# The down projection of two squared-ReLU MLPs as seven block products in place of eight, in a one-core Trainium2 kernel

## What is computed

```
D_MODEL = 1024; SEQ = 512; D_FF = 4 * D_MODEL
...
def mlp_sq_relu(h, w1, w2):
    return jnp.square(jax.nn.relu(h @ w1)) @ w2
...
        h = h + mlp_sq_relu(rms_norm_2(h, norm2[i]), mlp_w1[i], mlp_w2[i])
```

## Time and profile before

| | before |
|---|---|
| timed runs, median of 3 | 2932.26 us |
| lowest and highest | 2931.02 and 2935.89 us |
| the profiled execution: span | 2930.3 us |
| instructions | 51243 |
| PE busy (matmuls) | 2753.7 us, 94% |
| PEld busy (weight loads) | 2152.7 us, 73% |
| DVE busy | 1123.4 us, 38% |
| ACT busy | 916.9 us, 31% |
| POOL busy | 781.5 us, 27% |
| DMA | 397.00 MB, mean 135 GB/s |

### The profile page before, as it was taken

One profiled execution on the slowest core, in us unless ns is written; L12 is line 12 of the kernel. 1 busy time (PEld: TensorE's weight loads), 2 busy tenths in 40 slices (PEclk: granted clock), 3 DMA queues, 4 the chain that ended last, 5 costly groups with the idle time before them and its releaser, 6 DMA issues. The chain is left out here.

```text
span 2930.3 us, 51243 instructions
## 1 busy us (share of the span) xinstructions
PE 2753.7 (94%) x22943; PEld 2152.7 (73%) x22943; DVE 1123.4 (38%) x1554; ACT 916.9 (31%) x1458; POOL 781.5 (27%) x216
## 2 busy tenths in 40 slices
PE   7999989888989998888999999989999999999999
PEld 5877878778774333334899989987888888888887
DVE  5435765664552111114543475353211124431111
ACT  4133242343351000002355445543322232242222
POOL 2321332132120000001322332312444434434443
PEclk9999999999999999999999999999999999999999
DMA  7112201103165999996312221221332323322331
GB/s 276 53 33 63 65 4 63 62 3 106 48 244 223 424 426 427 427 427 257 128 58 73 72 86 54 78 72 58 101 101 88 99 87 101 99 88 89 100 101 58
DMA packets 171436, 397.00 MB, mean 135 GB/s; under 512 B 9519, under 2 KB 99604, under 8 KB 145876
## 3 DMA queue, kind: packets, MB, share of 16 engines
q1 hardware_dynamic: 170240, 390.34, 36.4%
q10 hardware_dynamic: 980, 3.40, 0.3%
HBM read 387.36 MB, written 4.19 MB: 134 GB/s over the span
## 5 line engine op out<-in xcount | busy, mean ns | idle before, releaser
L186 POOL TENSOR_TENSOR weight_ring_lo<-weight_ring,weight_hi 128x2048 fp32r<-128x2048 f32 (+1 forms) x144 | 656.9, 4562 | 1788.2 <-ACT weight_hi L175 1745.4
L175 ACT CAST weight_hi<-weight_ring 128x2048 fp32r<-128x2048 f32 (+1 forms) x144 | 271.4, 1886 | 550.1 <-PE late L244 309.9
L244 PE MATMUL late<-weight_hi,latT_hi 128*128 128x512 f32 x572 | 175.3, 429 | 0.0
L225 PE MATMUL late<-latT_lo,weight_hi 128*128 128x512 f32 x680 | 167.9, 389 | 0.0
L225 PE MATMUL late<-latT_hi,weight_ring_lo 128*128 128x512 f32 x680 | 167.9, 389 | 0.0
L225 PE MATMUL late<-latT_hi,weight_hi 128*128 128x512 f32 x680 | 167.9, 389 | 0.0
L244 PE MATMUL late<-weight_ring_lo,latT_hi 128*128 128x512 f32 x572 | 156.6, 396 | 0.0
L244 PE MATMUL late<-weight_hi,latT_lo 128*128 128x512 f32 x572 | 155.8, 394 | 0.0
L225 PEld LDWEIGHTS late<-latT_hi,weight_ring_lo 128*128 128x128 f32 x680 | 127.6, 188 | 26.5
L225 PEld LDWEIGHTS late<-latT_lo,weight_hi 128*128 128x128 f32 x680 | 127.6, 188 | 26.5
L225 PEld LDWEIGHTS late<-latT_hi,weight_hi 128*128 128x128 f32 x680 | 127.6, 188 | 26.5
(11 more groups left out here) (696 smaller groups left out, 5226.8 us busy)
## 6 DMA issues: line engine op xcount, KB each, us to landing
weight_ring<-in_mlp_w SPq DMA_DIRECT2D x64, 1024.0 KB, 5.3
weight_ring<-in_w_gate SPq DMA_DIRECT2D x41, 1024.0 KB, 15.2
weight_ring<-in_w_down SPq DMA_DIRECT2D x38, 1024.0 KB, 15.2
weight_ring<-in_w_up SPq DMA_DIRECT2D x36, 1024.0 KB, 12.7
weight_ring<-in_a_wqkv SPq DMA_DIRECT2D x36, 1024.0 KB, 5.0
weight_ring<-in_w_mod SPq DMA_DIRECT2D x24, 1024.0 KB, 5.7
weight_hi_spare<-in_w_up SPq DMA_DIRECT2D x16, 1024.0 KB, 12.5
weight_hi_spare<-in_w_down SPq DMA_DIRECT2D x16, 1024.0 KB, 15.1
```

Of the source, the lines that this page charges most:

```text
L175: self.nc.scalar.copy(self.view(self.hi[:, q % 2], p, True), self.view(self.slots[self.slot[p]], p, True)).then_inc(self.hi_ready, 1)
L186: self.nc.gpsimd.tensor_tensor(self.view(self.lo[:, s], p, True), self.view(self.slots[s], p, True), self.view(self.hi[:, q % 2], p, True) ...
L225: last = nc.tensor.matmul(dst, left(a, k), right(b, k), start=(a + b + k == 0), stop=(a == 1 and k == KD - 1))
L244: last = nc.tensor.matmul(dst, left(a, HK * r + k), right(b, k), start=(r + a + b + k == 0), stop=(r == 1 and a == 1 and k == HK - 1))
```

## The change

Waits, DMAs from memory and the up projection's matmuls stay as they were but for that. The same panels are loaded. The diff, cut to its core:

```
+    def add_item(self, split, shape, raw, lo, panel=None, formed=0, settled=0):
...
+            n = -(-shape[0] * shape[1] // HI_UNIT)
+            self.hi_at += -self.hi_at % n
+            units = [(self.hi_at + i) % HI_UNITS for i in range(n)]
+            self.hi_at = (self.hi_at + n) % HI_UNITS
+            item.hi = units[0] * HI_UNIT
+            item.hi_before = max(self.hi_holder[i] for i in units)
...
+    def form_seven(self, dve, group, behind):
...
+        V.tensor_tensor(t1, b12, b11, ALU.subtract).then_inc(self.formed, 1)
+        V.tensor_tensor(b12, b22, b12, ALU.subtract).then_inc(self.formed, 1)
+        dve.wait_ge(self.formed, group.n + 1)
+        V.tensor_tensor(t2, b22, t1, ALU.subtract).then_inc(self.formed, 1)
+        dve.wait_ge(self.formed, group.n + 3)
+        V.tensor_tensor(t4, b21, t2, ALU.subtract).then_inc(self.formed, 1)
...
+    def round_next(self, act):
...
+        if item.hi_before >= 0:
+            act.wait_ge(self.used, item.hi_before + 1)
...
+HI_UNIT = KD * PW // 2
+HI_UNITS = 4
...
+SEVEN = ((0, 0, 0, 0), (1, 1, 0, 0), (4, 0, 0, 1), (3, 1, 1, 1), (5, 0, 1, 1), (6, 1, 0, 1), (2, 0, 1, 0))
+FRESH = (0, 1, 3)
...
+    order = [("up", 0), ("up", 1)]
+    for n in range(N_DOWN):
+        order += [("up", u) for u in (2 * n + 2, 2 * n + 3) if u < N_UP] + [("down", n)]
...
+                pe.wait_ge(hidden, 2 * n + 2)
+                for i, (block_of, chain, _, _) in enumerate(SEVEN):
+                    w = st.take_split(pe)
+                    for s in range(2):
+                        if i >= 2:
+                            pe.wait_ge(drained, 14 * n + 2 * (i - 2) + s + 1)
+                        elif n:
+                            pe.wait_ge(drained, 14 * (n - 1) + 2 * (6, 5)[i] + s + 1)
+                        for a, b in ((0, 0), (0, 1), (1, 0)):
+                            for k in range(2):
+                                last = nc.tensor.matmul(acc[chain][s][:], hid_parts[a][:, (2 * n + k) % 4, block_of, s * P:(s + 1) * P], w[b][:, k, :],
...
+            def round_hidden(u):
+                act.wait_ge(combined, u + 1)
+                nc.scalar.copy(hid_hi[:, u % 4], hid[:, u % 4]).then_inc(rounded, 1)
...
+                for i in range(len(SEVEN)):
+                    act.wait_ge(st.used, at[t] + i + 1)
+                    st.round_behind(act, at[t] + i + 1, stop)
+                    if i == 1 and 2 * n + 3 < N_UP:
+                        round_hidden(2 * n + 3)
...
+            def combine(u):
+                a11, a12, a22, s1, s2, a21, s4 = (hid[:, u % 4, i] for i in range(7))
+                dve.wait_ge(squared, u + 1)
+                step.mark(V.tensor_tensor(s1, a21, a22, ALU.add))
+                first = step.n
+                step.mark(V.tensor_tensor(a21, a11, a21, ALU.subtract))
+                dve.wait_ge(step.sem, first)
+                step.link(dve, V.tensor_tensor(s2, s1, a11, ALU.subtract))
+                V.tensor_tensor(s4, a12, s2, ALU.subtract).then_inc(combined, 1)
...
+                u = 2 * n + 3
+                for i in range(len(SEVEN)):
+                    if u < N_UP and i < 3:
+                        (square, combine, lower)[i](u)
+                    for s in range(2):
+                        drain(n, t, i, s)
...
+                    if n + 2 == N_DOWN and i == 3:
+                        st.form_seven(dve, groups[n + 1], groups[n])
```

More of the change, by code:

```diff
@@ L109, in add_single_slots, with place @@
         return list(range(first, first + n))
-    def place(self, pieces, shape, split, n_slot, slot=None):
+    def place(self, pieces, shape, n_slot, ends, slot=None):
         p = len(self.panels)
@@ L144, in add_wide, with add_seven @@
                 self.add((w[r:r + D // 2, c:c + WIDE], 0), row=WIDE)
+    def add_seven(self, w, rows, turn):
+        t = len(self.items)
+        pair = [self.place(((w[rows:rows + D // 2, c:c + WIDE], 0),), (HK, WIDE, WIDE), SLOTS, end) for c, end in ((0, t + 1), (WIDE, t + 5))]
+        part = lambda buf, c, r: self.view(buf(self.slot[pair[c]]), pair[c])[:, r::2]
+        raw = lambda c, r: lambda: part(lambda s: self.slots[s], c, r)
+        low = lambda c, r: lambda: part(lambda s: self.lo[:, s], c, r)
+        own = lambda i: (lambda: self.own[:, i], lambda: self.own_lo[:, i])
+        shape = (HK // 2, WIDE, WIDE)
+        group = Buffers()
+        group.pair, group.first, group.n = pair, t, self.n_formed
+        group.b, group.t = [[raw(c, r) for c in range(2)] for r in range(2)], [own(i)[0] for i in (0, 1, 2 + turn)]
+        t1, t3, t2, t4 = range(group.n + 1, group.n + 5)
+        self.n_formed = t4
+        self.add_item(True, shape, raw(0, 0), low(0, 0), panel=pair[0], settled=t1)
+        self.add_item(True, shape, raw(0, 1), low(0, 1), panel=pair[0], settled=t4)
+        self.add_item(True, shape, *own(1), formed=t2, settled=t4)
+        self.add_item(True, shape, *own(0), formed=t1, settled=t2)
+        self.add_item(True, shape, raw(1, 0), low(1, 0), formed=t3, settled=t3)
+        self.add_item(True, shape, raw(1, 1), low(1, 1), panel=pair[1], settled=t2)
+        self.add_item(True, shape, *own(2 + turn), formed=t4, settled=t4)
+        return group
+    def form_seven(self, dve, group, behind):
+        V = self.nc.vector
+        (b11, b12), (b21, b22) = ([x() for x in r] for r in group.b)
+        t1, t2, t4 = (x() for x in group.t)
+        for p in group.pair:
+            dve.wait_ge(self.full[self.slot[p]], self.landed[p])
+        if behind is not None:
+            dve.wait_ge(self.used, behind.first + 4)
+        V.tensor_tensor(t1, b12, b11, ALU.subtract).then_inc(self.formed, 1)
[4 more added lines that the diff above has]
+        V.tensor_tensor(t4, b21, t2, ALU.subtract).then_inc(self.formed, 1)
     def view(self, buf, p, used=False):
@@ L3399, in _ @@
                             dense_behind(nc, up[0][0][:], left, right, lambda k: ahead.ready(pe, k))
                         else:
[L3401 to L3412, removed]
@@ new lines, in lower, with drain @@
+            def lower(u):
+                dve.wait_ge(rounded, u + 1)
+                V.tensor_tensor(hid_parts[1][:, u % 4], hid[:, u % 4], hid_hi[:, u % 4].bitcast(F32), ALU.subtract).then_inc(hidden, 1)
+            def drain(n, t, i, s):
+                _, chain, row, c = SEVEN[i]
+                if s:
+                    dve.wait_ge(st.used, at[t] + i + 1)
+                else:
+                    dve.wait_ge(filled, 7 * n + i + 1)
+                before = max([j for j in range(i) if SEVEN[j][2:] == (row, c)], default=-1)
+                if before >= 0:
+                    dve.wait_ge(drained, 14 * n + 2 * before + s + 1)
+                elif n:
+                    dve.wait_ge(drained, 14 * (n - 1) + 2 * max(j for j in range(7) if SEVEN[j][2:] == (row, c)) + s + 1)
+                d = x[:, 2 * row + s, c * WIDE:(c + 1) * WIDE]
+                last = V.tensor_tensor(d, d, acc[chain][s][:], ALU.add)
+                if n + 1 < N_DOWN or i < 5:
+                    last.then_inc(drained, 1)
+                else:
+                    last.then_inc(norm.x_ready if norm else added, 1)
```

236 lines of the change are left out of this document (122 added, 114 removed).

## The result

The changed kernel takes 3088.66 us, median of 4 runs (3086.19 to 3090.70), against 2931.64 us for the kernel before on the same chip: ratio 1.0532, 95% interval 1.0516 to 1.0547. It is slower by 157 us. The direction and the mechanism of the pauses were forecast, and the pauses are where the forecast had them; the time lies 3.7 us above the top of the range, and the term for the clock is the main reason.

A forecast was written before the change was run, and what follows sets the result against it. PE alone was taken to bound the MLPs. The profiled 2930.3 us, plus 111 for pauses less the saving and 11 for the clock, gave 3052, or 3054 with 2 for the median; range 3015 to 3085.

The forecast's parts named there:

- The saving: Both MLPs: 12 matmuls fewer in each of 16 down groups, at 2.72 us a group, 43.5 us less on PE.
- The high buffer: After down groups 0 to 5, the next up panel's cast waits for product 5's end; PE stands still 4.3 us.
- The turns: Down groups: DVE's four sums alternate with POOL's lowerings, product 1's drains queue behind, and product 3 starts 5.3 us late.
- the rival without alternation: Down groups: DVE waits once, then runs its four sums through; about 35 us more, 2967; chance 0.08, including anything between.
- 1.1 us at product 4: Down groups: ACT's hidden cast waits for the fourth sum, product 2's drains come later, and product 4 starts 1.1 us late.
- Groups 0 and 6: Each MLP: blocks 2 to 5 late by another 3.0 us in the first group; forming T blocks costs 3.9 at product 6.
- The forming, the loads, the drains' number, the other stages: T blocks formed at up panels' start, panel DMAs, 14 drains a group, and stages outside the MLPs: each adds nothing.
- The clock: Matmuls after 28 new PE pauses in both MLPs run partly at 1.2 GHz: 0.4 us each, +11 us.
- The ends I gave, 0 and 48: Bounds on the clock's cost in both MLPs: nothing, or 28 pauses at 1.7 us each, 48 us.
- the pauses less the saving: Both MLPs: PE's waiting, 77.4 us in each, less 21.8 saved in each; +111 us in all.
- one of the forecast's signs: In the changed profile, PE would be busy about 44 us less in all.
- the clock falls at every pause: Rival: the clock's cost after PE's pauses is the full 48 us; 3089, or 3091 by the median; chance 0.06.

The follow-up runs named there:

- units: Changed kernel with the high buffer's units for the seven blocks dealt 0,1,2,3,0,2,3 in place of 0,1,2,3,0,1,2; 3002.3 us, ratio 1.0244 to the kernel before.
- high_first: Changed kernel in which PE waits for an up panel's high part alone, for its low part only after 16 of 48 matmuls; 3022.70 us.
- clock_kept2: Changed kernel with small matmuls filling PE's pauses: 20 ahead of product 3, 15 ahead of even up panels and of product 6 of group 6; 3047.61 us.
- forming_more: Changed kernel with a fifth 128x1024 subtraction on DVE ahead of the T blocks of groups 0 to 6; 3091.42 us, ratio 1.0531 to the kernel before.
- clock_kept: Changed kernel with small matmuls filling PE's pauses: 36 ahead of product 3, 28 ahead of even up panels and of product 6 of group 6; 3099.12 us.
- no_turns: Changed kernel whose four sums of hidden blocks read one operand from PSUM, not SBUF (other sums, so another output); 3003.07 us.

## Why the prediction was wrong by a little

- **The saving, 43.5 us:** right as a price. A product takes 2.72 us at the full clock (in the changed kernel, 2779.44 to 2782.16), so the pace of the trace, 226.7 ns from start to start, was the one to take. The Trainium skill ("TensorE: Matmul & The Clock Gate", "Wait — 56ns, not 53.3ns?") gives 215.7 ns for 512 columns; the traces of both kernels show more, and the measurement decides.
- **The high buffer, 6 pauses of 4.3 us in an MLP:** right. They were 4.2 from the end of the last matmul's turn (2784.88) to 2789.05, six in each, and units and high_first remove them as reckoned.
- **The turns, 5.3 us at product 3:** right. 5.2 measured (2766.32 to 2771.49) in twelve of 14 groups; the sums took 1.34, 2.62, 2.58 and 2.44 us where the schedule had 1.3, 2.5, 2.5 and 2.6. Whoever asked first is next, as in the earlier trace rows, and the rival without alternation (2967) is out.
- **1.1 us at product 4:** not to be seen in the changed kernel, since product 3 on the lower level lasts 2.5 us longer and swallows it. Where product 3 runs at the full clock it is there: 1.05 us in each of 14 groups of clock_kept2, counted from the end of the turn.
- **Groups 0 and 6, 3.0 us more and 3.9 us:** right to some tenths. In clock_kept2 a group 0 waits 2.3 us at product 2 and 5.6 at product 3, 2.8 more than another group, and product 6 of a group 6 starts 3.6 after the end of product 5's turn, behind a filling of 3.5. In the changed kernel slow matmuls ahead of these pauses swallow part of them, so that 4.5 or 4.0 us at product 3 and 3.0 at product 6 are seen.
- **The forming, the loads, the drains' number, the other stages: nothing.** Right for the forming (forming_more). PE shows no wait for the loads, which isn't a test of its own. The other stages took 5.7 us more in the traced execution than before, and no run tells why; that is within the spread of the traces.
- **The clock, 0.4 us for each of 28 pauses, +11 us:** this is the step that failed. It measured 38 us in the MLPs of the traces, and 41 to 43 by the medians. The ends I gave, 0 and 48, held it, but I took a value near the lower end with the argument that part of the stretch lies in the pause and that the late drain swallows some. Both are true and too small. For one group: product 3 loses 2.46 us of which the pause at product 4 gives back 1.05, and the up panels lose 1.72: 3.1 us, where I had 0.8. Ten such groups, 1 to 5 of each MLP, are 31 us; the up panels behind the groups 0 (4.3) and product 3 of the groups 6 (1.4 each) bring it to 38. I also took the length of the stretch in the earlier trace rows, 3.4 us, as the longest it can be, though the one at product 3 is 6.8. And that the count of 28 comes out is luck: the two pauses at product 6 had no fall behind them, and two that I hadn't counted, of 2.3 us at product 2 of the groups 0, had one.

The sum with 38 in place of 11 is 3079 us, 3081 for the median, which is inside the range. Against the kernel before, the prediction had +122 us and the traces +154: 27 of the 32 between are the clock, 5.7 the stages outside the MLPs, and the pauses less the saving are right to 1 us. The timed medians have another 3 us, +157.

The same term made one of the forecast's signs false: PE's busy time was to fall by 44 us and rose by 29, though 192 matmuls were gone.

The rival "the clock falls at every pause" (3091) was nearly what happened, at a chance of 0.06, and the range's top should have taken it in.

## What to carry to other kernels

Before work is moved to an engine that has time to spare, look at what stands behind the new instructions in its queue, and whether another engine's instructions lock them out: four sums of 0.42 us lasted 8.9 us here because four lowerings of 2.4 came in between, and a PSUM drain was behind them. When a buffer is cut into finer pieces, follow one piece's last user to the next whole one's first use; the same seven blocks dealt to other units gave back 86 us of 157. And when PE's queue begins to have pauses of 4 us, price the matmuls that follow them at the lower clock before taking less.

## What the runs showed of the hardware that was not expected

- Each of the 24 pauses of 4.2 and 5.2 us on PE came with a stretch at the lower level. It was 6.8 us long and began within the pause at the twelve of 5.2 us and at three of the twelve of 4.2; at the other nine it was 3.4 us and began after the restart. Around 3 us it went either way: no fall behind the two of 3.0 us in the changed kernel, one behind nine of twelve of 3.1 us in units. The two MLPs ran at a mean of 0.91.
- Adding 20 and 15 small matmuls into pauses made the program 41 us faster (clock_kept2). Matmuls that nobody needs kept the clock at 1.00 in both fillings, but they paid only where they fitted the pause: 8.0 us of them in a pause of 5.2 (clock_kept) cost more than the clock does.
- A DVE addition or subtraction of 128x256 took 0.42 us with one operand in PSUM (no_turns) and 1.3 to 2.6 with both in SBUF, beside the same POOL subtractions; with POOL idle, 0.42 in SBUF too. The Trainium skill ("SBUF — State Buffer", "Who interferes with whom") says that only the latter contends; by that rule, the trace agrees. Who is next when both have more to do it doesn't say: here they alternate, and a group's four sums lose to four lowerings.
